# A hybrid decoder layer on eight cores: activations queued one block later in the first up-projection, one copy's wait moved, one weight load held back

## The reference, cut to what matters

```python
h = rms_norm(x, g_pre_mix) * (1.0 + scale_m) + shift_m
...                                    # two mixers and two gates give `merged`
mix = merged @ w_out
x = x + gate_m * rms_norm(mix, g_post_mix)

h = rms_norm(x, g_pre_ffn) * (1.0 + scale_f) + shift_f
up = causal_depthwise_conv(h @ w_up, conv_w, conv_b)   # width 3, (S, 2 * 5632)
a, g = jnp.split(up, 2, axis=-1)
y = (jax.nn.gelu(a) * g) @ w_down
x = x + gate_f * rms_norm(y, g_post_ffn)
```

## Time and profile before

| what | value |
|---|---|
| time, median of 3 runs | 1990.83 us (1989.57 to 1991.46) |
| the profiled execution | 1989.23 us |
| its span, slowest core (5) | 1987.7 us |
| spans of the 8 cores | 1979.2 to 1987.7 us |
| mean granted TensorE clock of the cores | 0.970 to 0.973 of full speed |
| PE busy | 1834.4 us, 92% of the span |
| DVE busy, ACT busy, POOL busy | 36%, 28%, 7% |
| w_out stage, A/B pass, C pass (starts, core 5) | 857, 996, 1080 us |
| first `up_block` matmul behind part C | 1126 us |

### The profile page before, as it was taken

How to read it: one execution, slowest core, us unless ns; L and a number is a source line. 1 busy time by engine, 2 the same in 40 slices (tenths; PEclk the granted TensorE clock), 3 DMA queues, 4 the chain that set the end, 5 groups by cost and what they waited for, 6 DMA issues and landing times.

```text
span 1987.7 us, 28298 instructions; the slowest of 8 cores (1979.2 to 1987.7 us)
## 1 busy us (share of the span) xinstructions
PE 1834.4 (92%) x11954; PEld 1114.7 (56%) x11954; DVE 715.7 (36%) x879; ACT 555.2 (28%) x777; POOL 142.3 (7%) x159
## 2 busy tenths in 40 slices
PE   2488999999999999989999799999999999999994
PEld 0144445666666666656655464566546664566564
DVE  0563003341111223313566451235423453234545
ACT  2323433110011111124566431243203431043321
POOL 0000000000000000002330000000000000000002
PEclk9689999999999999999999999999999999999997
DMA  9999679635978789675490763676357443653419
GB/s 250 168 155 143 108 103 140 95 55 85 136 111 127 116 141 149 103 142 145 117 184 1 117 101 58 104 115 100 61 99 117 75 72 59 104 85 69 81 20 150
DMA packets 108573, 216.66 MB, mean 109 GB/s; under 512 B 2720, under 2 KB 28832, under 8 KB 107168
## 3 DMA queue, kind: packets, MB, share of 16 engines
q0 software_dynamic: 99376, 187.18, 61.2%
q1 hardware_dynamic: 9072, 27.67, 4.4%
HBM read 376.84 MB, written 16.78 MB: 198 GB/s over the span
## 4 chain that ended last, share of the span: by engine, by line
PE 78%; DMA 9%; DVE 6%; ACT 3%; issue 3%; SPq 0%; POOL 0%; DVEq 0%; ACTq 0%; POOLq 0%
PE ps L276 59%; PE ps L522 6%; PE ps L1209 4%; PE ps L935 3%; DMA RC<-xT 2%; DMA RD<-w_out 2%; PE ps L420 2%; DMA RING<-w_ada 2%; DMA RING<-w_branch_a 1%; DMA RING<-w_in 1%; DVE R L994 1%; DVE R L992 1%; PE ps L331 1%; PE ps L1035 1%; ACT R L988 1%
## 5 line engine op out<-in xcount | busy, mean ns | idle before, releaser
L276 PE MATMUL ps<-RD,RING 128*128 128x342 bf16 (+1 forms) x3296 | 562.0, 330 | 0.9 <-DMA RING<-w_in 0.7
L276 PE MATMUL ps<-RC,RING 128*128 128x342 bf16 x3504 | 512.1, 308 | 7.5 <-ACT R L1077 7.5
L276 PEld LDWEIGHTS ps<-RD,RING 128*128 128x128 bf16 x3296 | 319.8, 97 | 231.3 <-issue 3.6
L276 PEld LDWEIGHTS ps<-RC,RING 128*128 128x128 bf16 x3504 | 339.4, 97 | 179.1 <-issue 9.6
L992 DVE SCALAR_TENSOR_TENSOR SC<-SC,vec 128x1024 f32<-128x1024 f32 x73 | 93.8, 1285 | 269.3 <-ACT SC L988 269.3
L1103 ACT ACTIVATE SC<-ps 128x1026 f32<-128x1026 f32 x73 | 74.9, 1026 | 372.5 <-PE ps L276 357.8
L522 PE MATMUL ps<-RING,RD 128*128 128x512 bf16 x576 | 127.9, 384 | 3.3 <-ACT RD L509 1.8
L276 PE MATMUL ps<-R,RING 128*128 128x342 bf16 (+1 forms) x784 | 125.9, 314 | 1.0 <-DMA RING<-w_branch_a 1.0
L276 PEld LDWEIGHTS ps<-R,RING 128*128 128x128 bf16 x784 | 75.9, 97 | 45.0 <-issue 2.4
L935 PE MATMUL ps<-RC,RING 128*128 128x342 bf16 x576 | 91.7, 312 | 7.1 <-DMA RING<-w_out 6.4
L522 PEld LDWEIGHTS ps<-RING,RD 128*128 128x128 bf16 x576 | 56.5, 99 | 73.3 <-issue 8.1
(11 more groups left out here) (166 smaller groups left out, 1475.8 us busy)
## 6 DMA issues: line engine op xcount, KB each, us to landing
RING<-w_ada POOLq DMA_DIRECT2D x24, 2048.0 KB, 19.0
RING<-w_in POOLq DMA_DIRECT2D x18, 2048.0 KB, 22.7
RING<-w_up POOLq DMA_DIRECT2D x15, 2048.0 KB, 16.7
RING<-w_down POOLq DMA_DIRECT2D x12, 1408.0 KB, 11.3
RING<-w_up POOLq DMA_DIRECT2D x8, 1536.0 KB, 14.2
R<-xP SPq DMA_DIRECT2D x6, 1368.0 KB, 14.0
RING<-w_branch_a POOLq DMA_DIRECT2D x4, 2048.0 KB, 23.5
R<-xT SPq DMA_DIRECT2D x3, 2304.0 KB, 29.7
```

The costliest lines, as they stand in the source:

```text
L276: e.matmul(o, lhsT=l, rhs=r, start=st, stop=sp),
```

## The change

1. In both passes the last step of `conv` (gelu on ACT, or the multiply on DVE) is returned as a function `finish` and put into the queues one block later: behind the next block's L988 (in A/B also behind the chain's piece there) and ahead of its L992. The last block of each pass is finished at the pass's end. In `up_block` it is called at once, so the order there stays.
2. In part C ACT's copy doesn't wait for the head copy any more; the first DVE tap (L992) does.
3. The load of w_up's first piece waits until w_out's last piece has landed.

```diff
@@ the loads
-        up_first = _load(("w_up", 0, KC, 0, UP_PCS[0][1]), "up", [hT_dead])
+        up_first = _load(("w_up", 0, KC, 0, UP_PCS[0][1]), "up", [hT_dead, wo[3][2]])
@@ conv
-        def conv(half, k, m, raw, cbuf, t_raw, cb_free_toks, c0, n, between=None):
+        def conv(half, k, m, raw, cbuf, t_raw, cb_free_toks, c0, n, between=None, head=None):
...
-                                                                op0=ALU.mult, op1=ALU.add), deps=[t_c0])
+                                                                op0=ALU.mult, op1=ALU.add), deps=[t_c0, head])
...
-            if half == 0:
-                t_o = P.op("act", lambda e: e.activation(out=dst, in_=cbuf, func=AF.Gelu_apprx_tanh), deps=[t_c2] + act_deps(k, m))
-            else:
-                t_o = P.op("dve", lambda e: e.tensor_tensor(out=dst, in0=dst, in1=cbuf, op=ALU.mult), deps=[t_c2] + act_ready[(k, m)])
-            return t_c2, t_o
+            def finish():
+                if half == 0:
+                    return P.op("act", lambda e: e.activation(out=dst, in_=cbuf, func=AF.Gelu_apprx_tanh), deps=[t_c2] + act_deps(k, m))
+                return P.op("dve", lambda e: e.tensor_tensor(out=dst, in0=dst, in1=cbuf, op=ALU.mult), deps=[t_c2] + act_ready[(k, m)])
+            return t_c2, finish
@@ the two passes
+        unfinished = []
+
+        def finish_last():
+
+            if unfinished:
+                finish, m, b = unfinished.pop()
+                t_o = finish()
+                cbf[b] = [t_o]
+                act_ready.setdefault((0, m), []).append(t_o)
@@ part A/B
-            t_c2, t_o = conv(half, 0, m, rawAB[b], cbAB[b], t_st, cbf[b], 0, NAB - 2, between=lambda: run_later(1))
+
+            def between():
+                run_later(1)
+                finish_last()
+            t_c2, finish = conv(half, 0, m, rawAB[b], cbAB[b], t_st, cbf[b], 0, NAB - 2, between=between)
             raw_free[b] = [t_c2]
-            cbf[b] = [t_o]
-            act_ready.setdefault((0, m), []).append(t_o)
+            unfinished.append((finish, m, b))
+        finish_last()
@@ part C
             t_st = P.op("act", lambda e, bk=bk, b=b: e.activation(out=rawC[b][:, 2:PN + 2], in_=bank(bk)[:, 0:PN], func=AF.Copy),
-                        deps=[tok, t_hd] + raw_free[b])
+                        deps=[tok] + raw_free[b])
             bank_free[bk] = [t_st]
-            t_c2, t_o = conv(half, 0, m, rawC[b], cbC[b], t_st, cbf[b], NAB - 2, PN)
+            t_c2, finish = conv(half, 0, m, rawC[b], cbC[b], t_st, cbf[b], NAB - 2, PN, between=finish_last, head=t_hd)
             raw_free[b] = [t_c2]
-            cbf[b] = [t_o]
-            act_ready[(0, m)].append(t_o)
+            unfinished.append((finish, m, b))
...
+        finish_last()
```

More of the change, by code:

```diff
@@ L1104, in up_block @@
             set_blk_free(i, [t_st])
-            t_c2, t_o = conv(half, k, m, stg[b], cb[b], t_st, cb_free[b], 0, TOK)
+            t_c2, finish = conv(half, k, m, stg[b], cb[b], t_st, cb_free[b], 0, TOK)
+            t_o = finish()
             stg_free[b] = [t_c2]
```

## The result

The changed kernel takes 1971.68 us (median of 10 runs) and the kernel before 1991.31 beside it; the ratio is 0.9906, interval 0.9894 to 0.9917, so it is 19 to 20 us faster. The prediction was 1971.7, with a range of 1967.5 to 1977.5.

The account below looks back on a forecast made before the run. PE was busy 92% of the span, so only its gaps could be won. Terms 7.1 + 10.0 + 1.5 + 0.5 = 19.1 us took 1989.23 to 1970.1, plus 1.60 for the median: 1971.7, range 1967.5 to 1977.5.

Parts of the forecast that it names:

- A/B: Part A/B: gelu one block later makes PE the pace in pair blocks; worth 7.1 us, bounds 2.5 and 9.0.
- the wait at block 12: Part A/B: the norm blocks' copies keep their 7.46 us ring, so PE waits 2.3 us ahead of block 12.
- 2.3 is nearer to the latter: minus 1.5: Block 12 of A/B: waits of 1.17 us cost no clock, 2.66 did, so a wait of 2.3 costs 1.5 us.
- the fall behind block 11: Kernel before, A/B: behind a 2.66 us wait, block 11 takes 6.26 us against 4.80 at a slower clock, 1.5 lost.
- The loop's price: A/B pair blocks, per block: PE 5.23 us, DVE 5.05, ACT 4.15, POOL 4.8 at most, so PE sets the pace.
- rival (1): A/B ring stays tied through chunk, POOL and squares; blocks keep about 6 us, A/B gives 2.5: 1976.3 us, chance 0.15.
- C: Part C: PE runs blocks in 35.3 us, then waits for w_up's next piece; L276 starts 10.0 us sooner, bounds 7 to 11.5.
- lands 17.3 later: 36.8: Part C: w_up's next piece, issued 19.5 us in, lands 17.3 later, so L276 starts at 36.8 instead of 46.8 us.
- the bound that I had set: Part C: 11.5 us gained if no load is waited for because it lands sooner.
- Clock behind L276: Matmuls behind part C: a wait of only 1.5 us costs no clock, so 1.5 us come back, bounds 0 and 1.5.
- The load: Holding back w_up's first block lands w_out's last piece sooner: 0.5 us taken, bounds 0 to 1.5.
- The reading of the landings: w_out's last piece and w_up's first block land a whole transfer apart, so only their edges can overlap: 0 to 1.5 us.

Follow-up runs that it names:

- E1: Kernel before with only part A/B's gelu one block later, part C and the load unchanged: ratio 0.9954 to the kernel before, A/B 65.3 us.
- E6: Changed kernel, with the loads of x's first part also waiting until w_out's third piece has landed: ratio 0.9907 to the kernel before.
- E8: Changed kernel with part C's blocks in the order 4 to 10, 0 to 3, 11 to 14: ratio 0.9889 to the kernel before, C 35.3 us.
- E9: The changed kernel run once more, as base for others on the same chip: ratio 0.9907 to the kernel before, median 1976.22 us.
- E10: Changed kernel with x's first part loaded behind w_out's fourth piece and w_up's first block behind x: ratio 0.9859 to the kernel before, median 1967.33 us.
- E2: Kernel before with only part C's two edits (later gelu, copy free of the head copy): ratio 0.9943 to the kernel before, 1980.44 us against 1993.49.
- E5: Kernel before with only the load of w_up's first block waiting for w_out's last piece: ratio 1.0002 to the kernel before.
- E3: Kernel before with only part C's gelu one block later, the copy still waiting for the head copy: ratio 0.9939 to the kernel before, C 43.2 us.
- E4: Kernel before with only part C's copy freed of the head copy, gelu staying in its own block: ratio 0.9960 to the kernel before, C 42.2 us.
- E7: Changed kernel with the chain's last five steps one a block in blocks 8 to 12 of A/B: ratio 0.9893 to the kernel before, A/B 62.7 us.

## Why the prediction was right, step by step

**A/B: right mechanism, 8.4 us for 7.1.** The A/B stage alone gave it (E1). Blocks 4 to 7 ran at PE's 5.23 us, block 8 started 1034.89 - 1004.69 = 30.2 us behind block 2 (30.3 predicted), and the wait at block 12 came, 2.40 us for 2.3. The step that was mis-sized is "2.3 is nearer to the latter: minus 1.5". Of the 44 cores with that wait in the profiles (4 of the changed kernel, 8 each of E1, E6, E8, E9, E10), 8 lost 1.6 to 1.7 us to the clock, 36 nothing: whether a wait of 2.4 us costs clock is a matter of chance. I had also read the fall behind block 11 of the kernel before as 1.5 us lost. On core 2 it didn't happen, and its A/B pass is 73.7 all the same: the ring set the pace, and the slow clock was hidden in it. Without the fall PE is done sooner with block 11 and waits 2.6 us ahead of block 12 instead of 0.9 to 1.2. That second wait can cost clock where nothing hides it. E2 to E5 have the A/B order of before; in their profiles and that of the kernel before, 12 of 40 cores kept the clock at block 11, and on 8 of these 12 it fell at block 12 and A/B took 75.4. Core 1 of E5 is one of them:

```profile
1061.02 4.80 PE L1044 MATMUL ps<-RC,RING 128*128 128x342 bf16 x32 [2.66 <-ACT R L1063]
1068.45 15.77 PE L1044 MATMUL ps<-RC,RING 128*128 128x342 bf16 x96 [2.62 <-ACT R L1063]
```

**The loop's price: too low, without effect.** DVE was to need 5.05 us a block; its turn is 5.50, since the two-column tail copy takes 0.68 beside POOL's adds, not 0.17, and the first tap 1.57, not 1.39. DVE has no idle time in this turn, so the ring is bound by it. That is rival (1) halfway. PE ran past it on the copies' lead; with 0.39 us left at block 7 and 0.27 lost a block, my estimate is that two more such blocks would have made the ring the pace again.

**C: right mechanism and right successor, 9.0 for 10.0 on core 5.** PE runs through C at 2.35 us a block, the copies wait for PE, and w_up's next piece is late next (E2, E8). The term "lands 17.3 later: 36.8" was 1.0 short there: 19.5 + 17.8 = 37.3, and 0.5 from landing to the first matmul. On the cores with early landing it was 11.5, the bound that I had set. That head copy and gelu are one ring, of which each edit alone wins little (3.6 and 4.6 us of 11.5), had not been said in the prediction; E3 and E4 showed it.

**Clock behind L276: 1.5, right on core 5, by chance.** The reason given was a wait of 1.5 us; the wait was 2.4. Behind waits of 2.17 to 3.60 us ahead of L276 (the changed kernel, E2, E6, E7, E9, E10) the clock fell on 8 of 16 cores (29.6 to 29.7 us for four blocks against 28.0), core 7 of the changed kernel among them; behind shorter ones, up to 2.09, on none of seven. So for the slowest core this term is a chance as well.

**The load: 0.5 predicted, 0.3 in core 5's stage, nothing in time or stages (E5).** The reading of the landings held: pieces on one queue land one after the other (in E10 18.2 and 28.8 us behind issues 0.9 apart). The Trainium skill says that each DMA engine takes descriptors in ring order (page "DMA: Bandwidth & Descriptors", section "Queues, rings and completion order"), and the trace agrees. Its rule that DMAs issued by different engines share the 16 DMA engines and interleave (section "Issuing engines are not separate DMA queues") had its place too, but at x's load from SP: E10 took that away and won 6.6 to 9.6 us a core.

**The sum on core 5.** The span fell by 22.0: 1.1 before w_out, 0.3 in w_out, 8.4, 9.0, 1.5 of clock, 0.3 in shorter waits for DVE's `modhl`, 1.5 at the end. The first and the last differ like that from execution to execution. The terms of the prediction are 19.2 of it, the medians differ by 19.6 (20.0 in the runs that the ratio counts), and 19.1 was predicted; that it is so close is partly luck, since A/B was put 1.3 too low and C 1.0 too high.

## What to carry to other kernels

When an in-order engine both frees PSUM and finishes work that waits for another engine, put the finishing behind the next block's copy; and look for every wait of the ring: opening one of two left the turn at 2.8 or 3.1 us here, opening both made it 2.35. Before taking the gain, ask what is issued by the stage's progress: here the next weights came 19.5 us into a 35 us stage with 17.8 us to land, and doing the blocks that free a slot first removed the wait. When a load is late, list all the queues' bytes in its time: the one on another engine's queue was the one to move, and it had to be moved behind all that is needed, not behind the first.

## What the runs showed of the hardware that I had not expected

- A DVE instruction that waits on DVE's own semaphore, for an instruction already done, made the turn 0.07 us longer (C 47.7 against 46.8 over 15 blocks).
- A copy of two columns on DVE that started 0.25 us behind the start of POOL's adds took 0.68 us; it took 0.16 to 0.17 where POOL was idle, and in the kernel before at the same place in the chain.
- The fall of TensorE's granted clock behind a wait of 2.4 us came on 8 of 44 cores, with the same matmuls ahead. Behind the wait of 2.66 us in the A/B pass of before it came on 28 of 40, and there it cost nothing, since the ring set the pace.
- The same 2 MB load behind block 7 of C took 13.4 to 13.6 us on four cores of the kernel before and 17.3 to 17.8 on the other four; in E9 it was 13.6 to 14.0 and 17.5 to 18.6. Of cores 0 and 1, 2 and 3, 4 and 5, 6 and 7 it was one of each, and the fast one was always the one that issued it first, by 4 to 7 us, each counted from its own first instruction. Which core of a pair that is changes from run to run. If being second is what makes the load slow, which no run tests, a core that is late is made later.
